# Softmax rows divided on GpSimd before the transposes, in place of scaling the product with V

## The reference, cut to what matters

```python
def attend(qb, qpos, cq=None):
    s = jnp.einsum('bhqd,bhkd->bhqk', qb, k, preferred_element_type=jnp.float32) * scale
    if cq is not None:
        s = s + (cq[..., :, None] - cum[:, :, None, :])
    s = jnp.where(key_pos[None, :] <= qpos[:, None], s, -jnp.inf)
    p = jax.nn.softmax(s, axis=-1)
    return jnp.einsum('bhqk,bhkd->bhqd', p.astype(v.dtype), v)
```

## Time and profile before

| What | Before |
|---|---|
| Median of 3 runs | 1502.51 us (1501.88 to 1503.54) |
| Span of the profiled execution | 1501.8 us |
| PE busy | 1480.5 us, 99% of the span |
| DVE busy | 838.5 us, 56% |
| ACT busy | 696.0 us, 46% |
| POOL busy | 3.6 us, 16 instructions |
| TensorE clock granted, mean | 0.999 of full speed |
| MLA attention on PE | about 836 to 972 us |
| FOX attention on PE | about 1166 to 1333 us |

### The profile page before, as it was taken

How to read it: one execution, slowest core, us unless ns; L and a number is a source line. 1 busy time by engine, 2 the same in 40 slices (tenths; PEclk the granted TensorE clock), 3 DMA queues, 4 the chain that set the end, 5 groups by cost and what they waited for, 6 DMA issues and landing times.

```text
span 1501.8 us, 26639 instructions
## 1 busy us (share of the span) xinstructions
PE 1480.5 (99%) x11599; PEld 1299.8 (87%) x11599; DVE 838.5 (56%) x1238; ACT 696.0 (46%) x1041; POOL 3.6 (0%) x16
## 2 busy tenths in 40 slices
PE   7999999999999999999999999999999999999998
PEld 7999999999999989988888677788899888778888
DVE  6487877764556556653336777542223665644343
ACT  6566768843342322223234766542223776742332
POOL 0000000000000000000000000000000000000000
PEclk9999999999999999999999999999999999999999
DMA  7222212134223223223234100222321111123222
GB/s 239 85 86 65 80 64 70 46 110 136 95 90 107 85 86 111 85 84 100 86 96 109 26 29 1 85 85 85 112 85 58 56 57 57 57 72 111 84 91 78
DMA packets 134535, 125.62 MB, mean 84 GB/s; under 512 B 24281, under 2 KB 132596, under 8 KB 134164
## 3 DMA queue, kind: packets, MB, share of 16 engines
q1 hardware_dynamic: 133940, 120.36, 25.7%
q0 software_dynamic: 464, 3.56, 0.7%
q10 hardware_dynamic: 16, 0.00, 0.0%
HBM read 119.66 MB, written 4.26 MB: 83 GB/s over the span
## 4 chain that ended last, share of the span: by engine, by line
PE 91%; DVE 4%; ACT 3%; issue 1%; DMA 0%; SPq 0%; DVEq 0%; ACTq 0%
PE PS L880 78%; PE PS L1219 3%; PE PS L1162 2%; PE PS L1184 2%; DVE wlo L1872 1%; PE PS L1167 1%; PE PS L1168 1%; ACT L1368 1%; PE PS L991 1%; PE PS L1169 0%; PE PS L1196 0%; ACT whi L1368 0%; DMA xt<-in_x 0%; PE PS L1188 0%; PE PS L947 0%
## 5 line engine op out<-in xcount | busy, mean ns | idle before, releaser
L880 PE MATMUL PS<-zhi,whi 128*128 128x258 f32 (+2 forms) x1856 | 489.2, 321 | 3.0 <-ACT hT L1368 1.4
L880 PE MATMUL PS<-zhi,wlo 128*128 128x258 f32 (+2 forms) x1856 | 476.9, 314 | 0.0
L880 PE MATMUL PS<-zlo,whi 128*128 128x258 f32 (+2 forms) x1856 | 475.9, 314 | 0.6 <-DVE zlo L1920 0.6
L880 PEld LDWEIGHTS PS<-zhi,whi 128*128 128x128 f32 x1856 | 307.4, 190 | 28.7 <-issue 1.9
L880 PEld LDWEIGHTS PS<-zhi,wlo 128*128 128x128 f32 x1856 | 306.2, 189 | 22.1
L880 PEld LDWEIGHTS PS<-zlo,whi 128*128 128x128 f32 x1856 | 305.5, 189 | 20.1 <-DVE zlo L1920 0.8
L1872 DVE TENSOR_TENSOR wlo<-raw,whi 128x2048 fp32r<-128x2048 f32 (+2 forms) x114 | 247.7, 2173 | 118.1 <-ACT whi L1368 117.9
L1368 ACT ACTIVATE whi<-raw 128x2048 fp32r<-128x2048 f32 (+2 forms) x114 | 207.4, 1820 | 149.6 <-DMA raw<-in_w_up 55.4
L1368 ACT ACTIVATE Pm<-PS,small 128x144 f32<-128x144 f32 (+3 forms) x128 | 68.8, 540 | 48.5 <-DVE small L2424 47.7
L2424 DVE TENSOR_REDUCE small<-PS 128x1 f32<-128x144 f32 (+3 forms) x128 | 63.4, 504 | 41.9 <-PE PS L1169 40.4
L880 PE MATMUL PS<-ghi,whi 128*128 128x512 f32 x176 | 69.6, 396 | 0.0
(11 more groups left out here) (357 smaller groups left out, 2075.7 us busy)
## 6 DMA issues: line engine op xcount, KB each, us to landing
raw<-in_w_in SPq DMA_DIRECT2D x50, 1024.0 KB, 5.2
raw<-in_w_up SPq DMA_DIRECT2D x22, 1024.0 KB, 5.0
raw<-in_w_out SPq DMA_DIRECT2D x8, 1024.0 KB, 5.0
raw<-in_w_down SPq DMA_DIRECT2D x8, 1024.0 KB, 5.1
raw<-in_w_br_mla SPq DMA_DIRECT2D x4, 1024.0 KB, 5.2
raw<-in_w_br_fox SPq DMA_DIRECT2D x4, 1024.0 KB, 5.1
raw<-in_w_down SPq DMA_DIRECT2D x4, 768.0 KB, 4.4
hspill<-hT SPq DMA_DIRECT2D x1, 2112.0 KB, 7.5
```

What stands on the lines that cost most here:

```text
L880: ins = mm(o_, l_, r_, start=first, stop=last)
```

## The change

GpSimd multiplies every tile of P in place by its reciprocal row sum, four instructions for each head, 128 in all. The reciprocals are taken by DVE in two steps: for tiles 0 to 2 at the end of iteration h, and for tile 3 at the start of iteration h + 1. `turn` of group 0 waits for GpSimd's fourth instruction of its head in place of ACT's fourth exponential. The spread reciprocals, `turn_sums`, ACT's copy of them and DVE's multiplication with them are gone; DVE copies the product from bank 7 as it is.

```diff
+            def divide(A):
+                for h in range(HEADS):
+                    for i in range(QB):
+                        pool.wait_ge(A.r_ready, 2 * h + 1 + i // 3)
+                        p_ = Pm[h % 2][:, ATT_OFF[i]:ATT_OFF[i] + ATT_N[i]]
+                        s_ = 4 * (h % 2) + i
+                        nc.gpsimd.tensor_scalar(p_, p_, rinv[:, s_:s_ + 1], None, ALU.mult).then_inc(A.divided, 1)
+            divide(mla)
+            divide(fox)
...
@@ PE: turn
-                    pe.wait_ge(A.p_exp, 4 * h + 4)
-                    if h and h % 2 == 0:
-                        pe.wait_ge(A.r_copied, h // 2)
+                    pe.wait_ge(A.divided, 4 * h + 4)
...
-            def turn_sums(A, p):
-                pe.wait_ge(A.r_ready, 2 * p + 2)
-                pe.wait_ge(A.pt_a, 4 * p + 4)
-                for i in range(QB):
-                    ins = tr(PS[:, 2, P * i:P * (i + 1)], A.rx[:, i, :], ident[:, :])
-                ins.then_inc(A.r_turned, 1)
...
                     if h >= 3 and h % 2 == 1:
-                        turn_sums(A, h // 2 - 1)
                         weigh(A, h // 2 - 1)
...
@@ ACT: attention
-                            if h >= 3 and h % 2 == 1:
-                                p = h // 2 - 1
-                                act.wait_ge(A.r_turned, p + 1)
-                                if p:
-                                    act.wait_ge(A.o_ready, p)
-                                A_(A.rs[:, :], PS[:, 2, :], ACT.Copy).then_inc(A.r_copied, 1)
-                            elif A is mla and h >= 2:
+                            if A is mla and h >= 2 and h % 2 == 0:
...
@@ DVE: attention
+            def row_root(A, h, tiles):
+                dve.wait_ge(A.p_exp, 4 * h + tiles.stop)
+                s = slice(4 * (h % 2) + tiles.start, 4 * (h % 2) + tiles.stop)
+                V.reciprocal(rinv[:, s], rowsum[:, s]).then_inc(A.r_ready, 1)
...
                 for h in range(HEADS + 2):
+                    if 1 <= h <= HEADS:
+                        row_root(A, h - 1, slice(3, 4))
                     project(h)
...
-                            if 1 <= h <= HEADS:
-                                x = h - 1
-                                dve.wait_ge(A.p_exp, 4 * x + 4)
-                                if x >= 2:
-                                    dve.wait_ge(A.r_turned, x // 2)
-                                s = 4 * (x % 2)
-                                tick(V.reciprocal(rinv, rowsum[:, s:s + 4]))
-                                settle()
-                                V.tensor_copy(A.rx[:, :, DV * (x % 2):DV * (x % 2) + DV],
-                                              rinv.unsqueeze(2).broadcast_to([P, QB, DV])).then_inc(A.r_ready, 1)
...
-                                dve.wait_ge(A.r_copied, p + 1)
-                                V.tensor_tensor(omla[:, p, :], PS[:, 7, :], A.rs[:, :], ALU.mult).then_inc(A.o_ready, 1)
+                                V.tensor_copy(omla[:, p, :], PS[:, 7, :]).then_inc(A.o_ready, 1)
...
+                    if h < HEADS:
+                        row_root(A, h, slice(0, 3))
```

More of the change, by code:

```diff
@@ L440, in build_program @@
         trig, e = at("trig", [P, 3, T], F32, e)
-        rxm, e2 = at("rxm", [P, QB, P], F32, e)
-        rsm, e2 = at("rsm", [P, SEQ], F32, e2)
-        r1, e2 = at("r1", [P, SEQ], F32, e2)
+        r1, e2 = at("r1", [P, SEQ], F32, e + 2 * SEQ * 4)
         assert e2 <= e + 3 * T * 4
@@ L446, in build_program @@
         nch, _ = at("nch", [P, T], F32R, e)
-        rsf, _ = at("rsf", [P, SEQ], F32, e)
         e += T * 4
@@ L469, in build_program @@
         assert e2 <= MIXOFF
-        rxf, _ = at("rxf", [P, QB, P], F32, N0 + 4 * T * 4)
         mtok, _ = at("mtok", [P, QB, D], F32, C + 16384)
@@ L477, in build_program @@
         lb, omlb, lbe, epst, fbias = small[:, 8:16], small[:, 16:24], small[:, 24:40], small[:, 40:41], small[:, 41:42]
-        negmax, rowsum, rinv, ssum, lbt = small[:, 48:56], small[:, 56:64], small[:, 64:68], small[:, 72:76], small[:, 80:96]
+        negmax, rowsum, rinv, ssum, lbt = small[:, 48:56], small[:, 56:64], small[:, 64:72], small[:, 72:76], small[:, 80:96]
         fsum, g12 = small[:, 96:112], small[:, 112:120]
@@ L561, in build_program, with __init__ @@
         class Attn:
-            def __init__(self, name, rx, rs):
-                self.rx, self.rs = rx, rs
+            def __init__(self, name):
                 self.s_done, self.m_ready = sem(name + "s_done"), sem(name + "m_ready")
                 self.p_exp, self.r_ready = sem(name + "p_exp"), sem(name + "r_ready")
-                self.r_turned, self.r_copied = sem(name + "r_turned"), sem(name + "r_copied")
+                self.divided = sem(name + "divided")
                 self.g_turned, self.pt_a, self.pt_v = sem(name + "g_turned"), sem(name + "pt_a"), sem(name + "pt_v")
                 self.o_done, self.o_ready = sem(name + "o_done"), sem(name + "o_ready")
-        mla, fox = Attn("mla_", rxm, rsm), Attn("fox_", rxf, rsf)
+        mla, fox = Attn("mla_"), Attn("fox_")
         hspill = nc.dram_tensor("hspill", [P, KT * T], F32, kind="Internal").ap()
@@ L1277, in _ @@
             pe.wait_ge(mla.pt_v, 2 * HEADS)
-            pe.wait_ge(mla.r_copied, KT)
             pe.wait_ge(z2_lo, KT)
@@ L1346, in _ @@
             pe.wait_ge(fox.pt_v, 2 * HEADS)
-            pe.wait_ge(fox.r_copied, KT)
             for k in range(3, KT):
```

## The result

| What | Before | After |
|---|---|---|
| Median | 1503.03 us (1501.88 to 1504.9) | 1557.62 us (1556.89 to 1561.09) |
| Ratio, 95% interval | 1 | 1.0364 [1.0349, 1.0379] |
| Span of the profiled execution | 1501.8 us | 1556.3 us |
| TensorE clock granted, mean | 0.999 | 0.985 |
| MLA attention, first scores to end of the last product with V | 135.2 us | 180.0 us |

The prediction was wrong: 1502.9 us, with a range up to 1513. Outside the two attentions nothing moved: +44.9 in MLA and +11.4 in FOX, less 1.8 us by which MLA began earlier, are the whole difference of the spans, 54.5.

A forecast was written before the change was run, and what follows sets the result against it. TensorE's work was taken to bound both attentions. Removed transposes -8.0 us, new waits +5.3 (even MLA iterations), +1.1 (iteration 1), +0.8 (iteration 16), +1.2 (FOX): +0.4, giving 1502.9 us, range 1497 to 1513.

The forecast's parts named there:

- The price of GpSimd's instruction: GpSimd's multiplication of 1344 columns a head in both attentions: 1.4 ns a column, 2.3 us a head (1.5 to 3.0).
- My upper bound of 2.2 ns: GpSimd's price per column if nothing of the 0.28 us select of 128 columns were fixed.
- The start of GpSimd: Delay between GpSimd's release by VectorE's reciprocal and its first multiplication, taken as 0.4 us.
- What the change removes: 64 TensorE transposes in both attentions, 16 groups at 0.50 us (0.42 to 0.59): 8.0 us gained (6.7 to 9.4).
- VectorE's lateness: MLA: query 0.3 us late in seven even iterations, 1.1 us more in iteration 1; 3.2 us even with fast GpSimd.
- The places of the wait: TensorE's first transposes: MLA even 2 to 14, 5.3 us; iteration 1, 1.1; 16, 0.8; FOX 14 and 16, 1.2.
- Nothing in the odd iterations of MLA: No new wait there: 3.1 us pass from the product with V's first load to the first transpose.
- Nothing in the other FOX iterations: No new wait outside FOX 14 and 16: at least three projection portions or the product with V stand in front.
- The slow GpSimd: Rival, both attentions: GpSimd at 2.2 ns a column makes waits of 15.4 us, +7.4, 1510 us; chance 0.13.
- GpSimd and VectorE hinder each other: Rival, at SBUF: one stands still for the other's whole instruction; 17.4 us of waits, +9.4, 1512 us; chance 0.22.
- The fast rival: GpSimd at 0.8 ns a column, its chain shorter than every gap; gains 4.8 us, 1497.7 us; chance 0.27.

The follow-up runs named there:

- the four forms: Changed kernel, P undivided; on an unawaited spare buffer GpSimd alternates by head: multiplication by a column, by a constant, copy, memset; 1497.66 us, timed once.
- with half the columns: Changed kernel with all its waits, but GpSimd multiplies only the first half of each tile's columns; 1508.81 us, 1.0038 of the kernel before.
- Without division: Changed kernel with the division of P left out and TensorE waiting for the fourth exponential as before; 1496.87 us, 0.9961 of the kernel before.
- the copies: Changed kernel with every wait and the order kept, but GpSimd copies each tile of P onto itself instead of multiplying; 1501.32 us, 0.9989.
- FOX with VectorE: Kernel before, MLA unchanged; only in FOX VectorE divides P ahead of its transposes; 1499.02 us, 0.9973 of the kernel before.
- the kernel with filled waits: Changed kernel, but TensorE transposes the identity, unread, ahead of selected waits for GpSimd; 1542.84 us, 1.0267 of the kernel before.

## Why the prediction was wrong

**The price of GpSimd's instruction: the step that failed.** I took 2.31 us a head and at most 3.0, from a memset and a select of 128 columns. Measured are 4.42 us undisturbed in FOX and 4.79 in even MLA iterations. The mistake was to read the select as the nearest row, since it "reads, computes and writes". As the four forms show, memset and copy cost 0.8 ns a column and a multiplication 2.5. My upper bound of 2.2 ns was no bound: it assumed that the select's rate was the worst that the engine has, and no row said so. The fixed part, 0.29 us for each of four instructions where I had 0.10, adds 0.76 us a head. The start of GpSimd went the other way, 0.10 us for my 0.40.

The Trainium skill, page "GPSIMD Engine Reference", section "Engine selection", says that elementwise work with one input runs at roughly line rate there; this holds for the copy (0.84 ns a column) and not for the multiplication (2.5). The same page of the Trainium skill, section "Key points", has VectorE about twice as fast for elementwise work; for this operation the factor is (1606 - 650) / (495 - 295) = 4.8 in the rate and 2.8 for a whole head (4.42 against 1.57 us).

**The consequence of a wait: the step that was missing.** My sum adds waits and knows nothing of the clock. At 0.75 us a wait that would have done: with half the columns, waits of 0.7 to 1.6 us left the clock at 1.00. At 2.64 us in every even iteration it did not, and 15 to 21 us came on top.

**What the change removes.** I took 0.50 us a group and named 0.42 as the value if the gap in front of the product stays. It stays: FOX gained 3.4 us over 8 groups with VectorE, 0.42 each. 16 groups are 6.8 us, not 8.0, inside my bounds.

**VectorE's lateness.** I had 0.3 us in each even iteration and 1.1 in the first, 3.2 in all. Without division MLA gained 2.6 us of 3.4, so the new order cost 0.8: its odd iterations are 0.45 us shorter than before and its even ones 0.1 longer. The rows above show why: the query starts 1.41 us after the last copy starts (892.64 to 894.05), and 1.30 before, 0.1 late and not 0.3. I had laid VectorE's instructions end to end, but each starts before the one ahead of it has ended: `zlo` 0.08 us after the start of a reciprocal of 0.16, the query 0.59 after the start of a `zlo` of 0.67. In iteration 1 VectorE was indeed late, its first multiplication 5.7 us after the first scores without division and 4.7 before, but TensorE's wait there grew only from 1.20 to 1.34 us. That wait was not for VectorE as I had read it: before, ScalarE was busy with other work (`fgt`, `zhi`) from 842.09 us until it began the exponential at 844.59.

**The places of the wait.** Even iterations 2 to 14 (seven times 2.6 to 2.9), iteration 1 (2.60, for GpSimd and not for VectorE's lateness), iteration 16 (4.99) and FOX's 14 and 16 (2.13 each) were right as places; FOX's 15 with 1.96 us was not among them. "Nothing in the odd iterations of MLA" was wrong above all for two of them, 3 and 11, with 2.66 and 2.04 us (5, 7 and 9 waited 0.2 each): GpSimd meets a low half of weights there and its 528 columns grow to 4.27 and 3.66 us. The trace of before had them, at 858.95 and 920.25 us, for instance

```profile
858.95 2.27 DVE L1872 TENSOR_TENSOR wlo<-raw,whi 128x2048 fp32r<-128x2048 f32 x1
```

but my description puts such work only in iterations 16 and 17. FOX's 15 is of the same kind: GpSimd's head took 6.17 us there, beside a low half at 1363.62. "Nothing in the other FOX iterations" was wrong beyond iteration 15 too: 4.5 us in seven waits of 0.4 to 0.9, which follow from the price.

**The rivals.** The slow GpSimd was the right mechanism at too small a price. That GpSimd and VectorE hinder each other was right as well, though smaller than the price: 0.4 us in most even iterations (4.79 against 4.42), where I had 0.67, and 2 to 3 where the low half of weights stands. In iteration 16 it made 2.6 us (7.04 for the head) where I had 2.9. Going through the heads, I estimate from GpSimd's time beyond 4.42 us, up to the length of each wait, that some 12 of the 42.3 us of waits come from the two engines meeting and 30 from GpSimd's own price; no run separates the two. The Trainium skill, page "SBUF — State Buffer", section "Who interferes with whom", says that a VectorE instruction with two SBUF inputs and a GpSimd instruction that reads SBUF exclude each other for a whole instruction; GpSimd's 3.54 us beside VectorE's unchanged 2.29 agrees, and here it is GpSimd that stands still. The fast rival, 1497.7, was tested by the copies, 1501.3, and fell too: FOX took the 167.6 us of the kernel without division, but MLA 136.3, 3.8 more than that kernel. Of these 2.26 are iteration 16, where I had named the meeting with the low half of weights under another rival and not here. So even a GpSimd at 0.8 ns a column would have been worth only 1.5 us.

**The range.** The half-column kernel shows that the rest of the working holds in the main: with the measured price and room, and with 1497 us for the kernel without waits, it gives the time within 1 us. The range's upper end rested on a price that no row of the trace bounded.

## What to carry to other kernels

Work handed to an engine for the first time has no price in the old trace; a row of the same engine with another operation is no bound for it, upward least of all. If the change is worth a few microseconds and hangs on that price, measure the instruction alone on a spare buffer first: one profile tells it. And where TensorE gets new waits of some 2 us or more, the cost is not only the wait: what follows it may run at half the clock, as it did here behind most of them but not all.

Here the same idea pays in the attention that has room and on the engine that has the rate: FOX with VectorE, 1499.0 us.

## What was not expected of the hardware

- GpSimd multiplies four-byte columns of 128 partitions at 2.5 ns each and 0.29 us fixed, and copies them at 0.84 ns. VectorE multiplies at 0.52 ns and 0.22 us fixed.
- When GpSimd's multiplication and a VectorE subtraction with two SBUF inputs overlapped, GpSimd's got longer by up to the subtraction's length (3.54 us for 1.61 beside one of 2.29), and VectorE's subtraction not measurably (672 ns in after against 669 for `zlo`). VectorE's multiplication that makes `nzt` did get longer, from 751 to 878 ns on average, and beside GpSimd's copies `zlo` did too, to 746.
- The granted clock does not follow the length of a wait alone. Waits of mostly 2.64 us in every second iteration took it to 0.89 over MLA; a wait of 2.26 us (the copies) or of 2.75 us (in the kernel with filled waits, which left iterations 3 and 11 unfilled) left it at 1.00. In FOX one of 2.15 us lowered it, with no wait over 0.9 us ahead of it there, and one of 2.14 us behind it did not. One of 3.30 us (half the columns) lowered it: matmuls of 512 columns behind it are first 0.40 and then 0.63 us long.

```profile
968.21 0.66 PE L1189 MATMUL PS<-ident,Pm 128*128 128x128 f32 x4 [3.30 <-POOL Pm L791]
...
969.16 0.40 PE L887 MATMUL PS<-zhi,wlo 128*128 128x512 f32 x1
...
969.74 0.63 PE L887 MATMUL PS<-zlo,whi 128*128 128x512 f32 x1
```

What exactly decides it stays open; no run here varied the length and the spacing of the waits alone.
